# Spreading the token rows of a PEER unit: four SBUF-to-SBUF transfers in place of 8 matmuls and 2 bank copies

## What is computed

```python
u_sel = u[e_idx]
v_sel = v[e_idx]
act = jax.nn.gelu(jnp.einsum('thkd,td->thk', u_sel, xb), approximate=False)
return jnp.einsum('thk,thkd->td', (gate * act), v_sel)
```

## Time and profile before

| | us |
|---|---|
| median of 3 runs | 4152.27 |
| the profiled execution | 4138.83 |
| its span, first to last instruction | 4137.0 |

### The profile page before, as it was taken

The page is one execution under the profiler, slowest core; times in us unless marked ns, Lnnn a source line. Parts: engine busy times, 40 slices in busy tenths (PEclk is TensorE's granted clock), DMA queues, the critical chain, the costliest instruction groups (busy, mean ns, idle before and its releaser), DMA issues.

```text
span 4137.0 us, 63615 instructions
## 1 busy us (share of the span) xinstructions
PE 3084.6 (75%) x22136; PEld 1883.1 (46%) x22136; DVE 2480.5 (60%) x6208; ACT 1628.4 (39%) x4703; POOL 1108.2 (27%) x1028
## 2 busy tenths in 40 slices
PE   7788987658989885758989887648989883444444
PEld 4576776325556563425556554315556561000001
DVE  2332317987458647677645547987558548955454
ACT  2214124534463534343453434534553533333333
POOL 0000001234333322224332331334333322443332
PEclk7769998769889997868889998768989995555555
DMA  7302435889989988988999996889989986999997
GB/s 255 115 1 89 125 117 211 328 344 354 364 333 419 388 323 308 353 343 342 366 370 361 367 399 245 346 333 354 399 332 419 394 301 237 397 404 421 421 418 323
DMA packets 247584, 1315.59 MB, mean 318 GB/s; under 512 B 21216, under 2 KB 35168, under 8 KB 116192
## 3 DMA queue, kind: packets, MB, share of 16 engines
q0 software_dynamic: 147456, 1073.81, 64.9%
q1 hardware_dynamic: 99808, 237.72, 16.0%
HBM read 1309.34 MB, written 2.10 MB: 317 GB/s over the span
## 4 chain that ended last, share of the span: by engine, by line
PE 30%; DMA 25%; DVE 20%; issue 7%; ACT 7%; PEld 7%; DVEq 2%; ACTq 1%; PEldq 1%; POOL 1%; POOLq 0%; SPq 0%
DMA row<-uv,e_idx 16%; DVE row L1525 6%; PE bank L615 6%; PE bank L655 5%; PE bank L669 4%; DMA weights<-w_in 4%; DMA weights<-w_ada 2%; PEld bank L669 2%; PEld bank L655 2%; PE bank L932 2%; PE bank L1000 2%; DVE reg L1422 2%; DMA weights<-w_out 1%; DVE reg L1417 1%; PE bank L848 1%
## 5 line engine op out<-in xcount | busy, mean ns | idle before, releaser
L1940 POOL DMA_INDIRECT row<-uv,e_idx x1024 | 1108.0, 1082 | 2995.1 <-PE bank L615 2091.7
L1525 DVE CUSTOM_DVE_ANT_0 row<-row,e_rep 128x1024 f32<-128x1024 f32 x1024 | 1239.9, 1225 | 747.4 <-DMA row<-uv,e_idx 695.9
L615 PE MATMUL bank<-row,e_diag 128*32 128x256 f32 x8192 | 831.3, 494 | 686.5 <-ACT e_diag L1096 651.3
L615 PEld LDWEIGHTS bank<-row,e_diag 128*32 128x32 f32 x8192 | 193.2, 122 | 1205.2 <-ACT e_diag L1096 968.1
L1092 ACT ACTIVATE e_ge<-e_dot 128x1 f32<-128x1 f32 x1024 | 206.2, 201 | 1203.7 <-DVE e_dot L1525 1185.6
L669 PE MATMUL bank<-hT,weights 128*128 128x256 f32 (+2 forms) x2176 | 536.6, 402 | 43.8 <-DMA weights<-w_in 29.1
L669 PEld LDWEIGHTS bank<-hT,weights 128*128 128x128 f32 (+2 forms) x2176 | 411.8, 195 | 169.7 <-issue 53.5
L655 PE MATMUL bank<-hT,weights 128*128 128x256 f32 x1536 | 366.5, 387 | 13.8 <-issue 12.8
L1096 ACT ACTIVATE e_diag<-mask,e_wg 128x32 f32<-128x32 f32 x1024 | 329.1, 321 | 75.4 <-issue 5.6
L1094 ACT ACTIVATE e_wg<-e_gate,e_ge 128x1 f32<-128x1 f32 x1024 | 301.5, 294 | 73.3 <-issue 3.1
L655 PEld LDWEIGHTS bank<-hT,weights 128*128 128x128 f32 x1536 | 280.5, 190 | 101.5 <-issue 66.1
(11 more groups left out here) (270 smaller groups left out, 3667.4 us busy)
## 6 DMA issues: line engine op xcount, KB each, us to landing
weights<-w_ada SPq DMA_DIRECT2D x48, 1024.0 KB, 7.9
weights<-w_mac SPq DMA_DIRECT2D x64, 768.0 KB, 8.4
weights<-w_in SPq DMA_DIRECT2D x44, 1024.0 KB, 8.9
weights<-w_mb SPq DMA_DIRECT2D x32, 768.0 KB, 8.4
weights<-w_out SPq DMA_DIRECT2D x16, 1024.0 KB, 14.6
weights<-w_pq SPq DMA_DIRECT2D x16, 1024.0 KB, 5.6
row<-uv,e_idx POOLq DMA_INDIRECT x1024, 10.2
weights<-w_in SPq DMA_DIRECT2D x8, 1056.0 KB, 5.2
```

The source lines that it names most:

```text
L615: last = mm(acc_ps[g % 2][c * QT:(c + 1) * QT, 0:2 * P], e_diag[:, n % RING, :], row[n % RING][:, D + c * 2 * P:D + (c + 1) * 2 * P], star ...
L1525: V.tensor_tensor_reduce(row[r][:, 0:D], row[r][:, 0:D], e_rep[g % 2], 1.0, 0.0, ALU.mult, ALU.add, e_dot[:, r:r + 1]).then_inc(dots, 1)
L1940: pool.indirect_dma_start(row[r], None, uv, bass.IndirectOffsetOnAxis(ap=e_idx[:, j:j + 1], axis=0)).then_inc(rows_landed[r], 16)
```

## The change

`spread` and its bank copies are gone, with the semaphore `spread_filled`, TensorE's waits for them and its 15 or so spread steps in each lap. `spread_copy(g, q)` is now one transfer from ScalarE's DMA queue: rows lo to lo + 31 of `e_h[t]` to partition group q of `e_rep[g % 2]`, 32 rows of 4 KB. For units after the first the four transfers stand at slots 8, 12, 16 and 20 of the unit before, as a step ahead of that slot's Gelu; the first waits until the dots that read this `e_rep` buffer are done. The four transfers of a lap's first unit are one step, after a wait for `h2_copied`. VectorE waits for all four by count (64 for each unit) before a unit's first dot. TensorE waits at slot 0 of a unit for `unit_out` of unit g - 2's result. ScalarE waits, before it overwrites `e_h`, that the transfers out of it have landed.

The digit strings are rewritten. Counted out, every slot step keeps its place on TensorE, ScalarE and VectorE; VectorE's order is unchanged. What moves on ScalarE, for a lap's first unit: in the first interleaved lap the fill stood at place 0 (ahead of the norm's root) and now stands at place 6, after the fourth of the eight additions of L1161, right ahead of slot 0's Gelu; in the second it stays at place 0, ahead of slot 0; in the third it moves from place 0 to place 2, after the root and before the first addition. In the tail it is ScalarE's first expert step, as before.

```diff
-SPREAD_AT, SPREAD_COPY_AT = (6, 10), (9, 13)
+SPREAD_AT = (8, 12, 16, 20)
@@ TensorE
-            def spread(g, x, b):
-                t, lo = g % UNITS // 4, QT * (g % 4)
-                for c in range(4):
-                    last = mm(acc_ps[b][c * QT:(c + 1) * QT, :], ident[:, lo:lo + QT], e_h[t][:, x * NB:(x + 1) * NB], start=True, stop=True)
-                last.then_inc(spread_filled, 1)
...
-                    if u < UNITS - 1 and s == SPREAD_AT[0]:
-                        if g:
-                            pe.wait_ge(unit_out, g)
...
-                        spread(g + 1, 0, (g + 1) % 2)
-                        yield True
...
-                    if s == 0:
-                        pe.wait_ge(spread_copied, 2 * g + 2)
+                    if s == 0 and g > 1:
+                        pe.wait_ge(unit_out, g - 1)
@@ ScalarE
-            def spread_copy(g, x, b):
-                act.wait_ge(spread_filled, 2 * g + x + 1)
-                A(e_rep[g % 2][:, x * NB:(x + 1) * NB], acc_ps[b][:, :], ACT.Copy)
-                act.drain().then_inc(spread_copied, 1)
+            def spread_copy(g, q):
+                t, lo = g % UNITS // 4, QT * (g % 4)
+                if g > 1 and q == 0:
+                    act.wait_ge(dots, USLOTS * (g - 1))
+                nc.scalar.dma_start(e_rep[g % 2][q * QT:(q + 1) * QT, :], e_h[t][lo:lo + QT, :]).then_inc(spread_copied, 16)
...
-                for x in range(2):
-                    spread_copy(UNITS * e, x, x)
-                    yield True
+                act.wait_ge(*G["h2_copied"].at(e, 2))
+                for q in range(4):
+                    spread_copy(UNITS * e, q)
+                yield True
...
+                    if u < UNITS - 1 and s in SPREAD_AT:
+                        if u == 3 and s == SPREAD_AT[0]:
+                            act.wait_ge(*G["h2_copied"].at(e, 4))
+                        spread_copy(g + 1, SPREAD_AT.index(s))
+                        yield True
...
+                    if lap:
+                        act.wait_ge(spread_copied, 64 * (UNITS * (lap - 1) + 4 * (t + 1)))
@@ VectorE
-                        dve.wait_ge(spread_copied, 2 * g + 2)
+                        dve.wait_ge(spread_copied, 64 * (g + 1))
```

More of the change, by code:

```diff
@@ L262 @@
[L262 to L265, removed]
@@ L271 @@
[L271 to L273 removed]
+        "0000000010020100020000010010010010001111101111110000220390000000p0000100000210000021000002000000000000100100110000000"
@@ new lines @@
+        "000000020000101000201100000010000010100000000000000010000000000000110000010001011010100100010011000000000000000200000"
+        "010010000110000010011011001000000100000010000010000000100100100100111111100001000000000002210131101011000010032011300"
+        "000010000000000301110000000000000000000010000130200003101201101110110110110110110111011011011011300100001100000020030"
+        "100000012100000000302100020200101011011012111010101001001300000000010100100101001004000000000010100100101200000001",
@@ new lines @@
+        "000000003000120001100000200000000000051000000000000011211000000000000301011000100220202100000003030001001000000000012"
+        "000112090000100110010004001000001001100000100000000001000000000010010000101001101000100010000010100000000000000010000"
+        "000000000110000010001011010100100011301000010000000001000000000001000010000010002011000100010000001001000001000000010"
+        "010011000010211110100000000000000024101211010110000100221011020010000000000003011100001000000000000000001000611110111"
@@ new lines @@
+        "101001010101010101010101010100101010101020001010101000001101100000000200000000000001050001001101101110110110110110110"
+        "0211110001110111000010002031111103010101012100000000000",
+        "0000100000200100110000010010010001000022101111000110220390000000p0000100000210000021000001000000000000110100100000000"
+        "100000020001001000101100010000010001100000000000000010000000000000110000010001011010100100010011000000000000000200000"
+        "010010000110000010011011001000000100000010000010000000100100100100111111100001000000000002210131101011000010032011300"
@@ L283 @@
-        "0110000417011001710110201000321000000000001000000000001122042040203020202020203010301040040205000005000000010221002210"
-        "10202030302020201004010000030100001100000006000000020010000000",
+        "000000200021003000001000211000100030210400301102030027v00133310030120232011100201110221202002121113112111021001010000"
+        "601100004170110026101202010003310000000000010000000000011220420402030203020302030103010400402050000050000000202310022"
+        "1010202030302020201004010000030100001100000006000000020100000000",
@@ new lines @@
+        "203340100000000202034000102001000000005010001010801000000161210010h00135140010221131011200101110221206001020203211311"
+        "012002000000510100005270110025110103100002310100000000000010001633040104010203020202010201010030004000003000000000100"
+        "00051100302030202020202007000100040100011100000007101310140000000000",
+        "002000000021003000103000000000100013030301301102030027v00133210022210221210200201110221202002121113112111021001010000"
+        "601100004170110026101202010004210000000000010000000000011220420402030203020302030103010400402050000050000000202310022"
@@ L285 @@
+        "1010202030302020201004010000030100001100000006000000020010000000",
     ),
     "DVE": (
[L287 to L295, removed]
+        "1021301050001020300011221122212122121220001000000100z0000000010300200300020000000020001010410201000010000000010001010"
@@ new lines @@
+        "30041000011000000001000211041030010101030100090000000e001100703010000006000000000000010000110110111030100110011011001"
+        "10011001100110011010110011001100110111012000101111011101111d020303020202010310031002061110000",
+        "9521000030150301010020000000800010110900000118110200000000000100i0000000010303010200020010000010002000410201000010000"
+        "0000100010103004100002111000000100021003103010101014000000090000000f0001007030100000060000000210100400201200200101101"
+        "100200200200200101100100200100100000011003010101180202020202020206010410120e3010000",
@@ L296 @@
+        "1111301050101010100121221122212122121220001000000100z0000000010300200210010000000020011100400300000110000000010001010"
+        "30041000011000000001000211041030010101030100090000000e001100703010000006000000000000010000110110111030100110011011001"
+        "10011001100110011010110011001100110111012000101111011101111d020303020202010310031002061110000",
     ),
@@ L587, in expert_steps @@
             def expert_steps(e):
-                pe.wait_ge(*G["h2_copied"].at(e, 2))
-                if e:
-                    pe.wait_ge(unit_out, UNITS * e)
-                for x in range(2):
-                    spread(UNITS * e, x, x)
-                yield True
                 for j in range(N_SLOT):
```

30 lines of the change are left out of this document (4 added, 26 removed).

## The result

| | before | after |
|---|---|---|
| median, us | 4152.91 (4147.49 to 4156.52, 4 runs) | 4209.80 (4205.18 to 4212.83, 4 runs) |
| ratio, 95% interval | | 1.0137 (1.012 to 1.0155) |
| profiled execution, span | 4137.0 | 4203.4 |
| TensorE matmul busy | 3084.6 | 3038.3 |
| ScalarE busy | 1628.4 | 1596.5 |

57 us slower, outside the forecast range of 4130 to 4198; the sign was right, the size was not. The page after, in the parts that answer to the earlier trace rows: the third part's queues (packets, MB, share of 16 engines) and the chain that ended last, by engine.

The account below looks back on a forecast made before the run. No single engine was taken to bound the kernel: TensorE and DMA nearly full in the laps, DMA full in the tail. Terms -15 + 2 + 7 + 10 + 7 + 2 + 0.5 = +13.5, say +14, gave 4166 us, range 4130 to 4198.

Parts of the forecast that it names:

- the sign: Whole kernel: slower by about 14 us; chances given were slower 0.50, faster 0.25, same 0.25.
- TensorE's relief: Interleaved laps: removing the spread matmul pieces of L578 that lie on the chain saves 15 us.
- ScalarE: Interleaved laps: four DMA issues a unit replace ScalarE's copies and drains, net +2 us; hidden in the tail.
- bytes in the tail: Tail, DMA engines full: five of seven units charged at 1.24 us each near the gathers' pace, +7 us.
- bytes in the laps: Interleaved laps: 24 units of 1.24 us make 30 us of engine time, between 6 and 27 felt, +10 us.
- heads: Starts of the laps and tail: first units' transfers land late, +7, 0, +2 and +0.5 us.
- the price of a unit's transfers: Laps and tail: a unit's 0.5 MB takes 1.24 us of all 16 engines at the gathers' pace.
- its rival: Laps, tail and heads: 32-partition transfers hold gathers for twice their bytes, +31 us, 4183; chance 0.16.
- The fourth rival: Laps: TensorE's freed pieces become waits for gathers or weights, relief 0, +29 us, 4181; chance 0.12.
- the first rival: Laps: TensorE's relief carries more, 45 us back, -26 us, 4126; chance 0.23.
- First head: First interleaved lap: slot 0's dot late because the last transfer lands 5.5 us after issue, +7 us, bounds 3 and 10.
- The tail's dot: Start of the tail: first dot begins 5.5 us behind the last transfer's issue, +0.5 us.

Follow-up runs that it names:

- e5: Changed kernel without the transfers of units 2 to 31 and with the first two units' fill issued early (stale rows), ratio to the kernel before 0.9989.
- e9: Kernel before the change with every spread matmul done twice, result unchanged: ratio to the kernel before 1.0019.
- e11: Changed kernel with transfers cut to 128 of 1024 columns from the third unit on, same four issues a unit: ratio to the kernel before 1.0036.
- e4: Changed kernel with each lap's first-unit transfers issued at the end of the lap before, ahead of routing and gathers: ratio to the kernel before 1.0114.
- e3: Changed kernel with half the columns (512 of 1024) in each transfer from the third unit on: ratio to the kernel before 1.0062.
- e7: Changed kernel with only each transfer's destination over every fourth partition, source still 32 neighbouring rows: 4156 us, one execution.
- e10: Changed kernel with two transfers of 64 neighbouring rows a unit in place of four of 32: 4202 us, one execution.
- e2: Changed kernel with one transfer of 128 rows a unit in place of four of 32, same 512 KB: ratio to the kernel before 1.0061.
- e6: Changed kernel with each 32-row transfer taking every fourth partition on both source and destination: ratio to the kernel before 1.0065.
- e8: Changed kernel with each transfer's source over every fourth partition, destination still 32 neighbouring rows: 4211 us, one execution.

## Why the prediction was wrong

| term | said | found | from |
|---|---|---|---|
| TensorE's relief | -15 | about -4 (-14 to +4); mirror +8 | e5, e9 |
| ScalarE | +2 | 0 to 10 | e11, issues of 514 ns |
| bytes in the tail | +7 | +19.7 | 681.1 against 661.4 |
| bytes in the laps | +10 | 22 to 32 by the medians, more by the traces | below |
| heads | +9.5 | about +10 | change less e4 |

The laps' figure is a remainder and not a measurement, so that the column adds up to the 57 us is no proof of it: e4 has no late heads and is 47 us over before; 19.1 of it are in the tail (680.5 us from first dot to last against 661.4); 28 are left for the laps, and the relief of about 4 is in them, so 32; less what the issues cost, 22 to 32. The two traces give 47.4 us for the laps, issues, relief and later heads included.

**The step that failed is the price of a unit's transfers,** the 1.24 us that the terms +7 and +10 both rest on. I took 1.24 us, the gathers' pace, with the reason that 4 KB rows are like the gathers' 8 KB rows. The measured 3.36 lies above even my upper bound of 3.0. Row length was the wrong likeness; e3, e7 and e10 show that the partitions written decide. The nearest rows could not show this, because every load, gather and store of the kernel before spans 128 partitions. The rule of the Trainium skill that I quoted did say it, and I gave its rival 16%. It belonged at the head of the list: it named exactly the property, 32 neighbouring partitions, that no row of the trace covered, while my likeness rested on one that a row covered but that did not matter. Even so its factor of two would have given 4183.

The price was not the whole error. With 3.36 us in my own sum, five units in the tail make 16.8 and a third of 24 units makes 27: -15 + 2 + 16.8 + 27 + 9.5 = +40, or 4193 us, still inside my range and 17 below the measured 4209.8. The relief, -4 in place of -15, adds 11, and the two tail units of the next paragraph 3: 4207.

**In the tail a second error added to it.** I charged five units of seven. The two units in which VectorE routes were 1.3 and 1.9 us longer too (94.34 against 93.07 and 91.00 against 89.06, from one dot of a slot 0 to the next): even where VectorE leads, the gathers run behind it closely enough.

**In the laps the share may have been right.** I let a third of the added engine time through. 24 units of 3.36 us are 81 us; by the medians up to 32 came through, 0.4, and by the two traces 47.4, 0.6. With the right price the term would have been 27. Which share holds stays open.

**The relief was read at full length from the chain.** Eighteen pieces of L578, 17 us, lie on the chain that ended last. Taken away they gave about 4, and doubled they cost about 8 (1 to 14). A piece on the chain bounds what it can give. Next to it stood the wait for the diagonal, which follows the gathers; and the matmuls that stayed took 24 us longer at a lower granted clock, which neither I nor any rival had in the sum. The fourth rival (relief worth nothing) is nearer to the truth than my term, though its waits are only part of the reason; the first rival is refuted.

**The heads came out in sum, not in place.** First head: 11.5 us later than the gather alone would allow (a wait of 12.62 against 1.08), where I had 7, since landing took 9.8 us and not 5.5. The tail's dot waited 3.2 us. In the second, VectorE waited 6.56, which I had rightly called covered in the main; in the third VectorE's wait ended on the gather. That e4 gives back 10 and not 22 fits: behind the second head TensorE waited for w_ada blocks anyway, until 1614.52 and 1623.14. That the three terms sum to what was found, 9.5 against about 10, is luck in part: the first was too small (7 against 11.5), the tail's too (0.5 against 3.2), and the third, for which I had 2, did not come.

No variant here that moves all the bytes by DMA comes near the kernel before. The relief is worth some 4 us, not clear of noise, and with it counted in, the cheapest transfers (e2, e6, e7, which move the wrong rows) still cost 24 to 27.

## What to carry to other kernels

Before giving work to the DMA engines, ask whether they are the resource that is full: here a small-looking queue of 1.3% cost almost all of the 57 us, and 62 us of TensorE time in the laps bought about 4. Price a transfer by its bytes and by the partitions that it writes, not by its row length: 32 or 64 neighbouring partitions cost 2.6 times the same bytes over all 128, and 32 partitions four apart cost no more than 128. When work is taken off TensorE, compare its busy time and granted clock too, since the matmuls that stay can take back part of the gain. A transfer that the head of a stretch waits for belongs ahead of the flood of gathers, where it hides.

## What was not expected of the hardware

The writing side alone is narrow: 32 neighbouring rows as a source cost nothing extra (e7, 1.3 us a unit), while spreading the source and keeping the destination narrow made it worse (e8, 4.8 against 3.36). While such a transfer is under way the DMA engines count as busy, 1.01 in both windows above, though 9 GB/s less move; a busy share of DMA does not tell useful bytes from engines held up. Queue shares over the four steady units show who is held up; before, after and e6:

```profile
q0 software_dynamic: 18433, 134.23, 101.0%
```

```profile
q0 software_dynamic: 18523, 134.86, 99.2%
q10 hardware_dynamic: 768, 2.10, 2.0%
```

```profile
q0 software_dynamic: 18472, 134.46, 99.4%
q10 hardware_dynamic: 768, 2.10, 1.6%
```

The transfers' own packets take 2.0% of 83.41, 1.7 us a unit. The gathers' packets (q0) take 82.7 us a unit where they took 80.9 before and take 80.9 in e6. So about half of the price is in the queue of the transfers, and the rest is in the gathers, which are slowed beside them; that is why q10's share looked so small. Four 128 KB transfers issued behind six gathers needed 9.8 us to land; eight stores of that size without gathers needed 1.8 each.
